# A reordered mixer front, key copies by SBUF transfers, and expert sums opened before the stream

## The chip, the core and the metric

The kernel runs on one core of one Trainium2 chip. Its time is the device time of one execution in microseconds (us), read as the median of a few runs. All data are float32. The engines named below are PE (TensorE, matrix products), DVE (VectorE), ACT (ScalarE), POOL (GpSimd) and SP (SyncE, which here only issues transfers).

## The reference

One decoder block over 256 tokens of 1024 features:

```
proj = rms_norm(x) @ w_in            # [u | q | k | v | q_idx | k_idx | w_idx | g_ssm | g_att]
q, k, q_idx, k_idx = rope(...)
y_ssm = S5 scan of u, gelu, y * sigmoid(y @ w_glu + b_glu)
score = sum over 16 index heads of relu(q_idx . k_idx) * w_idx     # causal, per 128-query block
sel   = top 64 keys of each query; softmax attention over them -> y_att
x = x + (sigmoid(g_ssm) * (y_ssm @ w_proj_ssm) + sigmoid(g_att) * (y_att @ w_proj_attn)) @ w_out
h = rms_norm(x); gates = softmax of the top 4 of 32 router logits
x = x + sum over 32 experts: gate * (clamped swiglu(h @ w_moe_in[e] + b_moe_in[e]) @ w_moe_out[e] + b_moe_out[e])
return rms_norm(x)
```

The expert weights are 32 x 12.6 MB, 403 MB of the 437 MB that the core moves.

## The kernel before, in words

**Layout.** Features lie on the partitions and tokens along the row in the mixer. One tensor `mem` of 24 slots of 8 KB per partition holds the mixer's tiles first and the weights of two experts later; `late`, `xs`, `table` and `bias_rows` lie beside it. PSUM has eight banks: 0 and 1 rotate among the "jobs" of the list `JOBS` (a job's products go to bank job number mod 2, and it waits until the job two before it is evicted); 2 and 3 take the scan's outputs and the attention's; 4 to 7 take scan inputs, index scores, logits, projections and at last the four sums of the expert stage (two token blocks by two feature halves).

**Order.** There is no scheduler: each engine's block is a program written out by hand, and semaphores order the engines. On PE, `x_job` is one chunk of `w_in` (256 columns, 64 matmul records), `score_job` four index heads of one query block, `logits(t)` the attention logits of block t, `turn_prob(t)` the transposes of its probabilities, `attend(t)` its products with v, `ps_job` a quarter of the projection of y_ssm. In the order of PE: `KK`, `QI0` to `QI3`, `VW`, `Q0`, `Q1`, `S0` to `S2`, then the three products `KR0` to `KR2` (L1092) that replicate each 32-row group of the rotated keys `kk` onto four groups of 32 partitions (`krep`), evicted by ACT; `S3` and `A0` with the eight score jobs between their steps; `A1`, `A2`, `logits(0)`, `GLU0/1`, `A3`, `logits(1)`, `PS0/1`, `turn_prob(0)`, `PS2/3`, `attend(0)`, `turn_prob(1)`, `attend(1)`; the attention projection (L1188), the output projection (`W0` to `W7`, L1211) with `aux` products (L1200) that turn the rows token-major and give router logits. DVE makes the scan, the rope, `y_raw` (L745), the index scores (L760, L763), `choose_keys` (eight rounds of max and match_replace, L776 and L777), `mask` (logits plus bias and row maxima, L791 and L794) and `probabilities`. ACT makes the gates, `exponentials` (L478) and most evictions.

**Expert stage.** `one_pass` treats each expert for up to 64 of its tokens: `gather` (L1236, products of `xs` with a one-hot), `gather_t` (L1244, transposes), the inner product (L1277, 64 records with the input bias of L1288), `scatter` of the expert before (L1253) into banks 4 to 7, the gates of the activation, and the outer product (L1325). Weights come in six loads of 2 MB per expert (`load_first` for the first two experts as slots come free, L359 in the loop: a load waits until the chunk two experts earlier has been used, `chunk_used`). In expert 30, L1303 adds the residual with `diag` (a diagonal of the norm's root); in expert 31, L1295 adds the output bias. A branch around further passes (L278) reads the largest number of tokens of an expert from `flag` (L277). Then the final norm is made from banks 4 to 7, and two transfers store the output.

## Time and profile before

| | |
|---|---|
| median of 3 runs | 1170.8 us (1169.01 to 1173.03) |
| the profiled execution's own time | 1169.42 us |
| its span | 1167.6 us |
| PE busy | 1118.3 us (96%), 5578 matmul records |
| DVE, ACT busy | 343.2 us (29%), 157.2 us (13%) |
| moved by the DMA engines | 437.01 MB, mean 374 GB/s |
| expert loads | 192 of 2048 KB |

The profile is of one execution. A busy PE is not PE at its peak, since records cover the wait for operands too. The profile's granted clock is a share of full speed: 1.00 is 2.4 GHz and 0.50 is 1.2 GHz. In a row of the chain or the timeline the first number is the start in us from the span's start and the second the duration; in brackets stands the idle time of the engine before it and what ended it.

### The profile page before, as it was taken

Reading aid. Unit: us, or ns where it says so; the run is one execution under the profiler, and the core shown is the slowest. Engines: PE = TensorE matmul, PEld = TensorE weight load, DVE = VectorE, ACT = ScalarE, POOL = GpSimd, SP = SyncE. Lnnn points to the kernel's source line nnn. Section 1 sums busy time; section 2 is a strip of 40 time slices with the busy share of each in tenths; the row PEclk is TensorE's granted clock in tenths of the full one; section 3 lists DMA queues with packets and bytes.
Section 4 is the critical chain, followed back from the end, with each engine's and each line's share of the span. In section 5 each row is a group of like instructions: output and inputs, shape, how many; then the busy total and the mean of one; then the engine's idle time right before and its main releaser. Section 6 shows DMA issues by size and latency. Waiting matters only on the chain.

```text
span 1167.6 us, 13800 instructions
## 1 busy us (share of the span) xinstructions
PE 1118.3 (96%) x5578; PEld 490.3 (42%) x5578; DVE 343.2 (29%) x760; ACT 157.2 (13%) x331; POOL 0.7 (0%) x7
## 2 busy tenths in 40 slices
PE   9999998989999999999999999999999999999995
PEld 8877786843333333333333333333333333333332
DVE  7999774221112221111111112211111111111112
ACT  2311433130001100010000001000000000000002
POOL 0000000000000000000000000000000000000000
PEclk9999998999999999999999999999999999999999
DMA  8343665589999999999999999999999999999992
GB/s 334 145 145 109 266 261 216 217 321 430 427 427 428 430 428 428 429 428 428 429 429 428 428 430 429 427 429 429 428 428 429 429 427 429 429 429 427 428 429 105
DMA packets 33434, 437.01 MB, mean 374 GB/s; under 512 B 3840, under 2 KB 3968, under 8 KB 5504
## 3 DMA queue, kind: packets, MB, share of 16 engines
q1 hardware_dynamic: 33120, 435.96, 89.1%
q10 hardware_dynamic: 288, 0.69, 0.2%
q8 instruction: 19, 0.31, 0.1%
q14 instruction: 7, 0.06, 0.0%
HBM read 435.58 MB, written 1.05 MB: 374 GB/s over the span
## 4 chain that ended last, share of the span: by engine, by line
PE 63%; DMA 22%; SPq 7%; DVE 6%; issue 1%; ACT 1%; DVEq 0%
PE ps L1277 25%; DMA mem<-in_w_moe 21%; PE ps L1325 13%; PE ps L1010 7%; SPq L359 7%; PE ps L1236 4%; PE ps L1253 3%; DVE mem L574 3%; PE ps L1211 2%; PE ps L1288 2%; PE ps L1188 1%; PE ps L1244 1%; PE ps L1310 1%; PE ps L1056 1%; PE ps L1107 1%
## 5 line engine op out<-in xcount | busy, mean ns | idle before, releaser
L1277 PE MATMUL ps<-mem,late 128*64 128x512 f32 x2048 | 458.2, 595 | 22.9 <-DMA mem<-in_w_moe 22.7
L1277 PEld LDWEIGHTS ps<-mem,late 128*64 128x64 f32 x2048 | 141.6, 137 | 330.7 <-issue 282.3
L1325 PE MATMUL ps<-mem,late 128*64 128x512 f32 x1024 | 226.8, 595 | 0.0
L938 DVE TENSOR_SCALAR late<-ps 128x512 f32<-128x512 f32 x32 | 22.1, 692 | 689.0 <-PE ps L1277 689.0
L1010 PE MATMUL ps<-mem 128*128 128x256 f32 x640 | 143.4, 382 | 0.0
L1010 PEld LDWEIGHTS ps<-mem 128*128 128x128 f32 x640 | 119.9, 190 | 21.0 <-issue 4.5
L1325 PEld LDWEIGHTS ps<-mem,late 128*64 128x64 f32 x1024 | 70.7, 137 | 133.3 <-issue 128.1
L537 ACT ACTIVATE late<-late 128x512 f32<-128x512 f32 x32 | 20.2, 630 | 514.9 <-DVE late L938 514.9
L1253 PE MATMUL ps<-late 64*128 64x512 f32 x256 | 63.6, 615 | 0.8 <-ACT late L544 0.8
L1236 PE MATMUL ps<-xs,late 128*64 128x512 f32 x256 | 63.5, 618 | 0.8 <-DVE late L574 0.8
L574 DVE TENSOR_TENSOR mem<-mem 128x1024 f32<-128x1024 f32 (+8 forms) x89 | 61.2, 729 | 6.5 <-ACT mem L429 3.7
L544 ACT ACTIVATE late<-ps 128x512 f32<-128x512 f32 x32 | 19.1, 597 | 230.7 <-PE ps L1325 230.7
L574 DVE TENSOR_TENSOR late<-late 128x128 f32<-128x128 f32 (+2 forms) x98 | 38.4, 419 | 6.5 <-ACT late L528 0.9
L1253 PEld LDWEIGHTS ps<-late 64*128 64x128 f32 x256 | 22.1, 186 | 41.8 <-issue 41.8
L1288 PE MATMUL ps<-bias_rows,late 32*64 32x512 f32 x256 | 34.8, 613 | 0.0
L574 DVE TENSOR_TENSOR late<-ps,vec 128x512 f32<-128x512 f32 x32 | 22.1, 692 | 41.4 <-PE ps L1244 41.4
L1236 PEld LDWEIGHTS ps<-xs,late 128*64 128x64 f32 x256 | 16.0, 138 | 43.1 <-issue 42.2
L574 DVE TENSOR_TENSOR mem<-ps,mem 128x1024 f32<-128x1024 f32 (+2 forms) x28 | 24.6, 914 | 18.1 <-PE ps L1188 16.9
L533 ACT ACTIVATE late<-ps 128x512 f32<-128x512 f32 x32 | 19.2, 599 | 79.5 <-PE ps L1236 79.5
L1211 PE MATMUL ps<-mem 128*128 128x256 f32 x128 | 28.8, 379 | 0.0
L1211 PEld LDWEIGHTS ps<-mem 128*128 128x128 f32 x128 | 24.0, 190 | 3.0
L1310 PEld LDWEIGHTS ps<-table,late 128*128 128x128 f32 x128 | 13.4, 140 | 28.1 <-issue 24.3
(161 smaller groups left out, 518.9 us busy)
## 6 DMA issues: line engine op xcount, KB each, us to landing
mem<-in_w_moe SPq DMA_DIRECT2D x192, 2048.0 KB, 42.4
mem<-in_w_mix SPq DMA_DIRECT2D x26, 1024.0 KB, 5.4
mem<-in_w_mix SPq DMA_DIRECT2D x2, 512.0 KB, 7.3
out<-xs SPq DMA_DIRECT2D x2, 512.0 KB, 3.1
late<-in_turn_w SPq DMA_DIRECT2D x1, 640.0 KB, 3.9
late<-in_mix_tables SPq DMA_DIRECT2D x1, 576.0 KB, 14.8
mem<-in_x_t ACTq DMA_DIRECT2D x1, 512.0 KB, 4.6
mem<-in_x_t SPq DMA_DIRECT2D x1, 512.0 KB, 5.8
```

Source lines behind the costliest of these rows:

```text
L359: sp.dma_start(place_of(half, n), expert_part(e, n)).then_inc(moe_in[half][n], 16)
L537: ac.activation(sig, gate_z, ACT.Sigmoid, scale=ALPHA).then_inc(sig_ok, 1)
L574: return ve.tensor_tensor(out_, a, b, op)
L938: ve.tensor_scalar(gate_z, z[:, 0], LIMIT, None, ALU.min).then_inc(z_gate, 1)
L1010: i = pe.matmul(b[:, m * T:m * T + T], slot[:, k, first_m + m, :], src[:, k, :], start=(k == 0), stop=(k == kt - 1))
L1211: i = pe.matmul(b[:, 0:T], wide(f"W{m // 2}")[:, k, m % 2, :], mixed[:, k, :], start=(k == 0), stop=(k == KD - 1))
L1236: i = pe.matmul(ps[64 * q:64 * q + SLOTS, 3, :], one_hot[:, t, :], xs[:, t, 512 * q:512 * q + 512], start=(t == 0), stop=(t == TT - 1))
L1253: i = pe.matmul(ps[:, 4 + 2 * t + q, :], gated_t[r, t * P:t * P + P], y_tok[r, :], start=opens, stop=False, skip_group_check=True)
L1277: i = pe.matmul(ps[r, n // 2, :], h_sel[:, k % 4, k // 4, :], w[:, 512 * n:512 * n + 512], start=(k == 0), stop=(k == KD - 1))
L1288: pe.matmul(ps[r, n // 2, :], chosen[g, n, :], b_in[g, :], start=False, stop=False)
L1310: i = pe.transpose(ps[:, 0, n * P:n * P + P], act[:, n * P:n * P + P], ident)
L1325: i = pe.matmul(ps[64 * q:64 * q + SLOTS, 2, :], act_tile(k), w[:, 512 * q:512 * q + 512], start=(k == 0), stop=(k == KF - 1))
```

## The change

1. The products `KR0` to `KR2` and their evictions go. SP copies the groups of `kk` by 12 transfers within SBUF, of 32 partitions by 2 KB, after `roped` 1 and before the load of `A2`; `score_job(0)` waits for the four of group 2, `logits(0)` for the other eight.
2. New order. The score jobs begin one step later and end in `A1`; `y_raw` comes after the scores on DVE; `logits(0)` and `logits(1)` come before and after `A2`; `turn_prob(0)` before `A3`; `attend(0)`, `turn_prob(1)` between the last `ps_job`s. `choose_keys(1)` is cut in two around `probabilities(0)`. The mask, exponentials and probabilities of block 1 go in two halves of four heads. All four `PS` evictions are made by DVE. `attend(1)` is in two halves, and the projection's first four outputs in two passes over k.
3. Opened sums. `aux` rows are kept unscaled in `raw`; four products with the identity put the residual into banks 4 to 7 before the expert loop (three of them before `picked_ok` is awaited, one after the first `gather_t`), so `diag` and L1303 go. The output bias goes into expert 1 (four products of 32 rows) and L1295 goes. `gates_turned` stands before `gather_t`. The load of chunk 5 waits for these.
4. Tail. `flag` is read at the start of the loop on each engine; ACT loads the root's table under the last outer product; the norm's mean and root are made per token block, and the last scaling of block 1 is shared by ACT and DVE.

The three places of PE's order that the prediction speaks of follow. First, behind `S2` (feature products are L1010 before and L1046 now; the key copies L1092; score jobs L1107 and L1135). Before:

```order
L1056 MATMUL ps<-mem 32x256 x16
L1010 MATMUL ps<-mem 128x256 x16
L1092 MATMUL ps<-mem,late 128x256 x6
L1010 MATMUL ps<-mem 128x256 x4
L1107 MATMUL ps<-mem 128x128 x8
```

Now:

```order
L1092 MATMUL ps<-mem 32x256 x16
L1046 MATMUL ps<-mem 128x256 x24
L1135 MATMUL ps<-mem 128x128 x8
L1046 MATMUL ps<-mem 128x256 x4
L1135 MATMUL ps<-mem 128x128 x8
```

The six key products are gone, and half of `S3` (eight instructions more in the row of feature products) comes ahead of the first score job; L1092 is now the scan's output.

Second, from the last scan output to the projection (L1124 and L1152 logits, L1136 and L1164 transposed probabilities, L1147 and L1175 products with v, L1188 and L1216 projection). Before:

```order
L1056 MATMUL ps<-mem 32x256 x16
L1010 MATMUL ps<-mem 128x256 x32
L1124 MATMUL ps<-mem 128x128 x16
L1010 MATMUL ps<-mem 128x256 x32
L1124 MATMUL ps<-mem 128x256 x16
L1010 MATMUL ps<-mem 128x256 x16
L1136 MATMUL ps<-table,xs 128x128 x8
L1010 MATMUL ps<-mem 128x256 x16
L1147 MATMUL ps<-mem 64x128 x8
L1136 MATMUL ps<-table,xs 128x128 x16
L1147 MATMUL ps<-mem 64x128 x16
L1188 MATMUL ps<-mem 128x256 x32
```

Now:

```order
L1152 MATMUL ps<-mem 128x128 x16
L1046 MATMUL ps<-mem 128x256 x16
L1152 MATMUL ps<-mem 128x256 x16
L1046 MATMUL ps<-mem 128x256 x16
L1164 MATMUL ps<-table,xs 128x128 x8
L1046 MATMUL ps<-mem 128x256 x32
L1175 MATMUL ps<-mem 64x128 x8
L1046 MATMUL ps<-mem 128x256 x8
L1164 MATMUL ps<-table,xs 128x128 x16
L1046 MATMUL ps<-mem 128x256 x8
L1175 MATMUL ps<-mem 64x128 x16
L1216 MATMUL ps<-mem 128x256 x32
```

Both blocks of logits now stand 16 or more feature products earlier, and the last `ps_job` stands between the transposes and the products with v of block 1.

Third, the start of the expert stage (L1219 and L1269 the slots' prefix sums, L1236 and L1286 gather, L1226 and L1276 the gates' transposes, L1244 and L1294 gather_t, L1262 now the opened sums). Before:

```order
L1200 MATMUL ps<-late,mem 128x160 x4
L1219 MATMUL ps<-late,table 128x64
L1220 MATMUL ps<-late,table 128x32
L1236 MATMUL ps<-xs,late 64x512 x4
L1244 MATMUL ps<-table,late 128x128 x4
L1226 MATMUL ps<-table,late 64x128 x2
L1227 MATMUL ps<-late,table 128x32
L1228 MATMUL ps<-late,table 128x32
L1277 MATMUL ps<-mem,late 64x512 x4
```

Now:

```order
L1241 MATMUL ps<-late,mem 128x160 x4
L1262 MATMUL ps<-mem,table 128x512 x3
L1269 MATMUL ps<-late,table 128x64
L1270 MATMUL ps<-late,table 128x32
L1286 MATMUL ps<-xs,late 64x512 x4
L1276 MATMUL ps<-table,late 128x128 x2
L1277 MATMUL ps<-late,table 128x32
L1278 MATMUL ps<-late,table 128x32
L1294 MATMUL ps<-table,late 128x128 x4
L1262 MATMUL ps<-mem,table 128x512
L1327 MATMUL ps<-mem,late 64x512 x4
```

Three opened sums stand where PE waited for the router, the gates' transposes moved ahead of `gather_t`, and the fourth sum stands ahead of the first inner product.

The diff, cut to what the prediction speaks of:

```diff
...
-JOBS = ["U0", "U1", "KK", "QI0", "QI1", "QI2", "QI3", "VW", "Q0", "Q1", "S0", "S1", "S2", "KR0", "KR1", "KR2", "S3",
-        "A0", "A1", "A2", "GLU0", "GLU1", "A3", "PS0", "PS1", "P0_0", "P0_1", "PS2", "PS3"] \
-    + [f"P1_{n}" for n in range(4)] + [f"W{m}" for m in range(KD)]
...
+JOBS = ["U0", "U1", "KK", "QI0", "QI1", "QI2", "QI3", "VW", "Q0", "Q1", "S0", "S1", "S2", "S3",
+        "A0", "A1", "A2", "GLU0", "GLU1", "P0_0", "P0_1", "A3", "PS0", "PS1", "PS2"] \
+    + [f"P1_{n}" for n in range(4)] + ["PS3"] + [f"W{m}" for m in range(KD)]
...
-            one_pass(0, 0)
-            eng.wait_ge(flag_ok, 1)
-            most = eng.value_load(flag[0:1, 0:1], min_val=0, max_val=T)
+            held = []
+            def most_tokens():
+                eng.wait_ge(flag_ok, 1)
+                held.append(eng.value_load(flag[0:1, 0:1], min_val=0, max_val=T))
+            one_pass(0, 0, most_tokens)
+            most = held[0]
...
+            sp.wait_ge(roped, 1)
+            for n in (2, 0, 1):
+                for a in range(4):
+                    sp.dma_start(krep[32 * a:32 * a + 32, n], kk[32 * n:32 * n + 32]).then_inc(krep_in[n], 16)
+            load("A2")
...
-            sp.wait_ge(rstd_ok, 1)
+            sp.wait_ge(opened, 1)
+            sp.wait_ge(x_norm, TT)
             load_first(5)
...
-            relus(0, 1, 2)
+            relus(0, 1)
             gate("S", gate_s, V_BG, 3)
             ac.wait_ge(roped, 3)
-            relus(3, 4, 5, 6)
+            relus(2, 3, 4, 5)
             gate("A", gate_a, V_BG + KD, 0)
-            relus(7)
...
+            relus(6, 7)
...
+            ready(ACT.Exp)
+            exponentials(0, 1, 0, NH)
...
-            exponentials(0)
+            prob_turned(0)
+            ready(ACT.Exp)
+            for n in range(2):
+                exponentials(1, 2 + n, 4 * n, 4 * n + 4)
...
-            for n in range(2):
-                evict(f"PS{n}", p_ssm[:, 2 * n:2 * n + 2, :], pair)
-            prob_turned(0)
-            exponentials(1)
-            attended(0)
+            attended(0, 1, 2, slice(0, 4))
             prob_turned(1)
-            attended(1)
+            attended(1, 2, 3, slice(0, 2))
+            attended(1, 3, 2, slice(2, 4))
...
-                for t in range(TT):
-                    ac.activation(at(10 * SW + P * (TT * m + t), P), b[:, t, 0:P], ACT.Square,
-                                  accum_out=stat[:, 64 + KD * t + m:65 + KD * t + m]).then_inc(squared1, 1)
-                ac.activation(xs[:, :, m * P:m * P + P], b[:, :, 0:P], ACT.Copy).then_inc(tok_ok, 1)
+                ac.activation(raw[:, :, m * P:m * P + P], b[:, :, 0:P], ACT.Copy).then_inc(tok_ok, 1)
...
-            ac.wait_ge(var_f_ok, 1)
-            ac.activation(stat[:, 4:6], stat[:, 2:4], ACT.Sqrt).then_inc(root_f_ok, 1)
-            ac.wait_ge(rstd_f_ok, 1)
+                if n % 2:
+                    t = n // 2
+                    ac.wait_ge(mean_f_ok, t + 1)
+                    ac.activation(stat[:, 4 + t:5 + t], stat[:, t:t + 1], ACT.Sqrt, scale=1.0 / D,
+                                  bias=stat[:, 46:47]).then_inc(root_f_ok, 1)
+            ac.wait_ge(rstd_f_ok, 2)
             ac.wait_ge(under_gains, 4)
-            ac.activation(final[:, 1, :], final[:, 1, :], ACT.Copy, scale=stat[:, 7:8]).then_inc(out_ready[1], 1)
+            ac.activation(final[:, 1, 0:512], final[:, 1, 0:512], ACT.Copy, scale=stat[:, 7:8]).then_inc(
+                out_ready[1], 1)
...
+            ve.wait_ge(y_done, 4)
+            for a in range(KS):
+                i = ve.scalar_tensor_tensor(y_raw[:, a, :], u_in[:, a, :], vec[:, V_D + a:V_D + a + 1],
+                                            ps[:, 2 + a // 2, (a % 2) * T:(a % 2) * T + T], ALU.mult, ALU.add)
+            i.then_inc(y_raw_ok, 1)
+            choose_keys(0, 0, NSEL // 8)
+            mask(0, 0, NH)
+            choose_keys(1, 0, 5)
+            probabilities(0, 1, 0, NH)
+            choose_keys(1, 5, NSEL // 8)
             ve.wait_ge(*evicted("GLU1"))
             ve.wait_ge(*evicted("GLU0"))
             tt(y_ssm, y_gelu, glu_g, ALU.mult).then_inc(y_ssm_ok, 1)
-            choose_keys(1)
-            probabilities(0)
-            ve.wait_ge(*evicted("PS1"))
-            ve.wait_ge(*evicted("PS0"))
-            tt(p_ssm[:, 0:4, :], p_ssm[:, 0:4, :], gate_s[:, 0:4, :], ALU.mult)
-            mask(1)
+            for n in range(2):
+                mask(1, 4 * n, 4 * n + 4)
+            for n in range(2):
+                probabilities(1, 2 + n, 4 * n, 4 * n + 4)
             ve.wait_ge(rout_in, 16)
             tt(turn_w[:, :, P:P + NE], turn_w[:, :, P:P + NE],
                vec[:, V_G2:V_G2 + KD].unsqueeze(2).to_broadcast([P, KD, NE]), ALU.mult).then_inc(w_gain, 1)
-            for n in (2, 3):
+            for n in range(4):
                 ve.wait_ge(rot_done, JOB[f"PS{n}"] + 1)
...
                 ins.then_inc(route_ok, 1)
             def gates_out():
-                for t in range(TT):
-                    ins = ve.tensor_scalar(diag[:, t, :], ident, stat[:, 4 + t:5 + t], None, ALU.mult)
-                ins.then_inc(diag_ok, 1)
...
                 ve.tensor_copy(stat[:, 62:63], stat[:, 60:61])
             passes(ve, one_pass)
-            ve.tensor_copy(stat[:, 63:64], stat[:, 60:61]).then_inc(tile_ok, 1)
...
             for n, bank_free in ((1, None), (0, (squared, 1)), (3, (sum_ok, 1)), (2, (squared, 3))):
+                if n == 3:
+                    ve.wait_ge(squared, 2)
...
                    ALU.mult).then_inc(under_gains, 1)
+            ve.wait_ge(root_f_ok, 1)
+            ve.reciprocal(stat[:, 6:7], stat[:, 4:5]).then_inc(rstd_f_ok, 1)
...
-            ve.tensor_scalar(stat[:, 2:4], stat[:, 0:2], 1.0 / D, EPS, ALU.mult, ALU.add).then_inc(var_f_ok, 1)
-            ve.wait_ge(root_f_ok, 1)
-            ve.reciprocal(stat[:, 6:8], stat[:, 4:6]).then_inc(rstd_f_ok, 1)
+            tt(stat[:, 1:2], stat[:, 50:51], stat[:, 51:52], ALU.add).then_inc(mean_f_ok, 1)
             ve.wait_ge(rstd_f_ok, 1)
             ve.wait_ge(under_gains, 4)
             ve.tensor_scalar(final[:, 0, :], final[:, 0, :], stat[:, 6:7], None, ALU.mult).then_inc(out_ready[0], 1)
+            ve.wait_ge(root_f_ok, 2)
+            ve.reciprocal(stat[:, 7:8], stat[:, 5:6]).then_inc(rstd_f_ok, 1)
+            ve.wait_ge(rstd_f_ok, 2)
+            ve.tensor_scalar(final[:, 1, 512:D], final[:, 1, 512:D], stat[:, 7:8], None, ALU.mult).then_inc(
+                out_ready[1], 1)
...
-            pe.wait_ge(roped, 1)
-            for n in range(3):
-                b = job(f"KR{n}")
-                r = slice(32 * n, 32 * n + 32)
-                for half in range(2):
-                    i = pe.matmul(b[:, half * T:half * T + T], sel[r, :], kk[r, half, :], start=True, stop=True)
...
-                    pe.wait_ge(*evicted("KR2"))
+                    pe.wait_ge(krep_in[2], 64)
...
             def turn_prob(t):
-                pe.wait_ge(prob_ok, t + 1)
                 for n in range(2 * (t + 1)):
...
+            def scores_from(first):
+                return lambda step: score_job(first + step) if 0 <= first + step < 8 else None
+            x_job("S3", between=scores_from(-1))
+            x_job("A0", between=scores_from(3))
             y_out(3)
-            x_job("A1")
-            pe.wait_ge(tables_in, 16)
+            x_job("A1", between=scores_from(7))
+            logits(0)
             x_job("A2")
-            logits(0)
+            logits(1)
             chunk_arrived(pe, "GLU")
             pe.wait_ge(gelu_ok, 1)
             for n in range(2):
                 feature_job(f"GLU{n}", y_gelu, KS, 2 * n, deep("GLU"))
+            pe.wait_ge(tables_in, 16)
+            turn_prob(0)
             x_job("A3")
-            logits(1)
             pe.wait_ge(y_ssm_ok, 1)
             ps_job(0)
             ps_job(1)
-            turn_prob(0)
+            attend(0, 2, range(NH))
             ps_job(2)
+            turn_prob(1)
             ps_job(3)
-            attend(0)
-            turn_prob(1)
-            attend(1)
-            pe.wait_ge(att_out, 2)
-            pe.wait_ge(row_max, 2)
-            for m in range(KD):
-                if m % 4 == 0:
-                    chunk_arrived(pe, f"PA{m // 4}")
-                if m >= 4:
-                    pe.wait_ge(gated_a, m - 3)
+            attend(1, 3, range(4))
+            pe.wait_ge(att_out, 1)
+            attend(1, 2, range(4, NH))
+            def project(m, ks):
                 slot = deep(f"PA{m // 4}")
-                for k in range(KS):
+                for k in ks:
                     i = pe.matmul(ps[:, 4 + m % 4, (m // 4) * T:(m // 4) * T + T], slot[:, k, m % 4, :],
                                   y_att[:, k, :], start=(k == 0), stop=(k == KS - 1))
-                i.then_inc(proj_done, 1)
+                return i
+            chunk_arrived(pe, "PA0")
+            pe.wait_ge(row_max, 3)
+            pe.wait_ge(att_out, 2)
+            for m in range(4):
+                project(m, range(2))
+            pe.wait_ge(att_out, 3)
+            for m in range(4):
+                project(m, range(2, KS)).then_inc(proj_done, 1)
+            chunk_arrived(pe, "PA1")
+            for m in range(4, KD):
+                pe.wait_ge(gated_a, m - 3)
+                project(m, range(KS)).then_inc(proj_done, 1)
...
+            open_sums(0, 0)
+            open_sums(1, 0)
+            open_sums(0, 1)
...
-                            pe.matmul(ps[:, 4 + k, :], gates_t[r, t * P:t * P + P], b_out[r, :], start=False,
-                                      stop=False, skip_group_check=True)
+                        if out_bias and k == 0:
+                            pe.wait_ge(gates_t_ok, 1)
+                            for n in range(4):
+                                r = slice(NE * n, NE * n + NE)
+                                pe.matmul(ps[:, 4 + n, :], gates_t[r, n // 2 * P:n // 2 * P + P], b_out[r, :],
+                                          start=False, stop=False, skip_group_check=True)
                     if not head:
-                        scatter(j - 1, opens=opens)
-                        if adds:
-                            pe.wait_ge(diag_ok, 1)
-                            for t in range(TT):
-                                for q in range(2):
-                                    pe.matmul(ps[:, 4 + 2 * t + q, :], diag[:, t, :], xs[:, t, 512 * q:512 * q + 512],
-                                              start=False, stop=False, skip_group_check=True)
+                        scatter(j - 1)
                     if not tail:
                         gather(j + 1)
...
+                if isinstance(c, int):
+                    gates_turned()
                 gather_t(first)
                 if isinstance(c, int):
-                    gates_turned()
+                    open_sums(1, 1).then_inc(opened, 1)
                 pairs = c * (NE // 2)
...
+                body(first + 1, pairs, 1, out_bias=isinstance(c, int))
+                if most_tokens:
+                    most_tokens()
                 with pe.Fori(1, NE // 2 - 1) as m:
                     for odd in range(2):
                         body(2 * m + (first + odd), m + pairs, odd)
-                body(first + NE - 2, pairs + NE // 2 - 1, 0, adds=isinstance(c, int))
+                body(first + NE - 2, pairs + NE // 2 - 1, 0)
                 body(first + NE - 1, pairs + NE // 2 - 1, 1, tail=True)
                 pe.wait_ge(gated_t_ok, first + NE)
                 scatter(first + NE - 1, first_sum_ok)
...
```

## Rows read from the trace of the kernel before

**Rows 1.** Timeline of SP's queue, first issue of the expert loop.
```profile
258.72 37.19 SPq L359 DMA_DIRECT2D mem<-in_w_moe  x10
```

**Rows 2.** Windows: each engine's busy us, granted clock, DMA share, GB/s.
```profile
300.00:700.00 400.00, 400.00 (x1924) 135.19 (x1926) 71.16 (x171) 34.62 (x58) 0.00 (x0) 1.00 1.01 428
188.00:192.00 4.00, 3.45 (x16) 2.67 (x14) 0.00 (x0) 2.31 (x4) 0.00 (x0) 0.50 1.01 426
248.00:250.00 2.00, 1.93 (x6) 0.78 (x8) 0.99 (x6) 0.96 (x3) 0.00 (x0) 0.50 1.05 451
```

**Rows 3.** The chain that ended last: start us, us, what; its middle.
```profile
181.02 4.05 ACT xs L478 x16
...
1056.54 48.09 DMA mem<-in_w_moe
1104.68 3.65 PE ps L1277 x16
```

**Rows 4.** The same chain, from expert 30's residual to the end.
```profile
1110.25 3.63 PE ps L1303 x8
...
1124.12 1.72 PE ps L1277 x8
...
1126.85 1.05 PE ps L1295 x2
...
1136.66 7.04 PE ps L1277 x32
...
1147.89 7.08 PE ps L1325 x32
...
1157.73 2.28 issue
```

**Rows 5.** PE's timeline before the expert stage.
```profile
109.27 2.94 PE L1092 MATMUL ps<-mem,late 32*128 32x256 f32 x12
...
134.47 1.93 PE L1056 MATMUL ps<-mem 128*32 128x256 f32 x32
...
182.92 1.09 PE L1147 MATMUL ps<-mem 128*64 128x128 f32 x16
187.68 3.77 PE L1136 MATMUL ps<-table,xs 128*128 128x128 f32 x16 [3.67 <-DVE xs L574]
192.23 3.71 PE L1147 MATMUL ps<-mem 128*64 128x128 f32 x32 [0.78 <-ACT mem L429]
196.62 14.08 PE L1188 MATMUL ps<-mem 128*128 128x256 f32 x64 [0.69 <-ACT mem L488]
...
246.63 0.43 PE L1219 MATMUL ps<-late,table 128*128 128x64 f32 x2 [3.64 <-DVE late L865]
...
248.07 3.51 PE L1236 MATMUL ps<-xs,late 128*64 128x512 f32 x8 [0.81 <-DVE late L574]
```

**Rows 6.** DVE's timeline, from y_raw to the mask of block 1.
```profile
136.54 1.66 DVE L745 SCALAR_TENSOR_TENSOR mem<-mem,vec,ps 128x256 f32<-128x256 f32 x4 [8.10 <-PE ps L1056]
...
148.57 0.29 DVE L574 TENSOR_TENSOR mem<-mem,late 128x128 f32<-128x128 f32 x1
...
156.74 1.22 DVE L794 TENSOR_REDUCE stat<-xs 128x8 f32<-128x1024 f32 x1
...
160.67 0.42 DVE L574 TENSOR_TENSOR mem<-mem,late 128x256 f32<-128x256 f32 x1
...
169.66 0.43 DVE L574 TENSOR_TENSOR mem<-mem,late 128x256 f32<-128x256 f32 x1
...
176.38 2.28 DVE L791 SCALAR_TENSOR_TENSOR xs<-ps,mem 128x2048 f32<-128x2048 f32 x1
```

**Rows 7.** ACT's timeline: the last relu of the scores.
```profile
134.60 1.02 ACT L464 ACTIVATE mem<-ps 128x1024 f32<-128x1024 f32 x1 [0.27 <-PE ps L1107]
```

**Rows 8.** The branch of PE around further passes: ns min/median/max, start.
```profile
L278 PEldq COMPARE_BRANCH  x1: 3312/3312/3312, 1156.6 to 1156.6; - x1
```

**Rows 9.** DMA issues: count, KB each, median us from issue to landing.
```profile
mem<-in_w_mix SPq DMA_DIRECT2D x26, 1024.0 KB, 5.4
```

169 lines of the change are left out of this document (87 added, 82 removed).

## The prediction

> **What bounds the kernel now.** I read the windows first, then the chain that ended last, then PE's timeline up to the expert stage, then DVE's. In the window 300 to 700 us both PE and the DMA engines are full, the latter at 428 GB/s [rows 2]. The chain tells which of them sets the end: near it, PE waits for a load of expert weights that lands at 1056.54 + 48.09 = 1104.63 us [rows 3]. A load of 2.097 MB at 428.5 GB/s takes 4.89 us. The loop's first load is issued at 258.72 [rows 1]; the one of 1104.63 (chunk 3 of expert 30) is the 172nd, and 258.72 + 172 x 4.89 = 1100, plus some 4 us from issue to landing. So from the first used chunk on the stream is back to back: the end is the moment at which PE uses its first chunk, plus a stream of fixed length, plus what PE does after the last landings. Whatever brings the first inner product forward by one microsecond brings the end forward by one; work taken from PE in the middle brings nothing; work taken from PE behind 1104.63 counts as far as the loads let it.
>
> Behind 1104.63 the chain is PE's own until the norm [rows 4]. The loads of expert 31 land 4.89 apart: its chunk 0 at about 1119.3, chunk 3 at 1134.0, chunk 5 at 1143.8.
>
> Ahead of the stream PE is without a gap up to 174 us, and then loses time in one place: it waits 3.67 for the probabilities of block 1, then its granted clock is 0.50 (1.2 GHz), then it waits 0.78 and 0.69 for evictions [rows 2, 5]. A second place is the router: a wait of 3.64, then a first gather at half clock [rows 2, 5]. DVE, on whose work the first wait rests, sat idle for 8.10 us before `y_raw` [rows 6].
>
> **Front: keys and order.** The key products leave PE: 2.9 us [rows 5]. Their replacement is 12 transfers of 64 KB. SP is free for them at about 101 us, when the first rope ends, behind the load of `A1`. The nearest row is 1 MB in 5.4 us [rows 9]; 12 x 64 KB is 0.79 MB, so I take 6 to 8 us: landed at 107 to 109. The first score job wants group 2 at 109.3 plus half a chunk, 16 records of 0.22 = 3.5 (0.22 is 14.08 / 64 [rows 5]), so 113; the logits want the rest at 141. The next load of SP, `A2`, waits for `S2` until 109.3 anyway. Cost nothing, with about 4 us of cover; beyond that each microsecond costs one. Bounds: 0, and the row of 5.4 us for each transfer, one after another: 12 x 5.4 = 65, the last landed at 166, 25 us too late for `logits(0)`. I take 0, because transfers overlap in the queue: a load that is 48.09 us under way [rows 3] has others landing every 4.89.
>
> DVE is idle from 136.54 - 8.10 = 128.4 because `y_raw` stands ahead of the scores. Now the scores start there and end 2.6 (a quarter of the 10.4 between 138.2 and 148.57 [rows 6]) after the last relu. That relu started at 134.60 [rows 7]; it gains 2.9 by the keys but the last score job now comes behind y_out (1.93, [rows 5]) and a quarter of `A1` (1.8): it starts at 135.5, ends at 136.5; scores end at 139.1, `y_raw` (1.66) at 140.8. Selection and mask of block 0 took from 148.57 to 156.74 + 1.22 = 157.96 [rows 6], 9.4 us; so they end at 150.2, 7.8 us earlier. PE reaches `logits(1)` at 148.8 and waits 1.4 there for bank space: the one new wait. DVE then needs 9.4 (160.67 to 170.09 [rows 6]) for the selection of block 1, 1.5 for `probabilities(0)`, 1.2 for y_ssm, 4.9 for two mask halves: 167.3. The exponentials (4.05 for eight heads [rows 3], now two times 2) overlap the halves, and the last probabilities are ready at 170.8. PE asks for them at 179.7, so the wait of 3.67 goes, with 9 us of cover. Evictions of ACT lie beside PE; I walked them one by one, and they leave 0.3 us in `turn_prob(0)` and 0.8 in `turn_prob(1)`.
>
> Without the long wait the clock should stay at 2.4 GHz. At 1.2 GHz the products with v took 3.71 for 32 records, against 1.09 for 16 at 2.4 GHz, so 2.2 for 32: 1.5 lost; the transposes took 3.77, of which 1.4 by the same share [rows 2, 5]. Sum up to the projection: 2.9 (keys) + 3.7 (wait) + 2.9 (clock) + 1.5 (two eviction waits) - 1.4 - 1.1 = 8.5 us; the projection starts at 188.1 instead of 196.62 [rows 5]. The first four outputs of the projection come in two passes, but DVE's gating still keeps ahead of PE. All loads that wait on these events shift with them.
>
> **Front: opened sums.** Three of the four identity products (0.9 each, as L1303 took 3.63 for four [rows 4]) fill the 3.64 us of waiting for the router; they cost nothing and keep PE at work. The gather then should take 1.9, not 3.51: 1.6 gained. But `gates_turned` (0.75) now stands ahead of `gather_t` and must wait for four gate copies, and the fourth sum (0.9) stands ahead of the first inner product, beside the eviction by DVE (0.7) that this waits for: 0.6 back. Net 1.0 us; between -0.2 (clock still low) and 1.6.
>
> The Trainium skill (TensorE: Matmul & The Clock Gate, "What's actually happening") says that the throttled clock is the default and activity releases it. This trace agrees in direction: 0.50 after the idle stretches, 1.00 before them [rows 2]. By it the gather would get the 1.6; a trace of an engine with short gaps there is not in this profile, so the sum above keeps the rest as a bound.
>
> The load of chunk 5 is issued 9 us later in relation to the gather, but it is the sixth of an expert and wanted 20 us later; it lands just when the stream begins, so no hole opens. The output bias adds 1.0 to expert 1, and the reading of `flag` some 0.8 on PE, both in the part of the stream where PE is ahead of the loads: nothing.
>
> **End of the stream.** L1303 (3.63) and the four L1295 (4 x 1.05) leave PE behind 1104.63, 7.8 us. PE would be ready for expert 31 at 1124.12 - 3.63 = 1120.5, its chunk 0 has landed at 1119.3. Steps of 1.8 bring it to chunk 3 at 1132.7, which lands only at 1134.0; two steps (3.65 [rows 3]) more, and the inner product ends at 1137.65, not 1136.66 + 7.04 = 1143.70 [rows 4]. 6.0 us gained, 1.8 kept by the loads. Chunk 5 (1143.8) is wanted at 1145.4: it doesn't bind. Bounds: 4.5 if landings are 1.5 later than I extrapolate, 7.8.
>
> **Tail.** The wait of 2.28 us before the last two sums [rows 4] looks like the reading of `flag`, but the long part is PE's branch, 3.31 us from 1156.6 [rows 8], and the branch stays. Only the read ahead of it goes, some 0.7: between 0 and 0.7, as the branch may wait for the last products; I take 0.4. If the branch was long only because of the read, 2.3. The divided last scaling and the mean per block give 0.2. Together 0.6.
>
> **Sum.** 8.5 + 1.0 + 6.0 + 0.6 = 16.1 us. The profiled execution took 1169.42: 1153.3. It lies 1.4 below the median of the runs, 1170.8, which would give 1154.7. I predict 1154.0.
>
> **Rivals.**
> - The chain through DVE and ACT is later than I walked it (evictions in the new order block a bank, halves cost more than their share): the front gives 4 instead of 8.5, so 1158.5. For it: PE has only two rotating banks. Against it: 9 us of cover in the longest chain.
> - The clock falls anyway, in the new wait at 149 or a later one. Before, a half-clock stretch followed a wait of 3.67, and the following work cost 2.9 more [rows 5]; with a full chunk of feature products at half clock it costs up to 5: 1159. Against it: no wait above 1.4 remains.
> - The stream does not start earlier: the loads of the first two experts, which come free with the mixer's tiles, are late. Then only 6.6 stand: 1164. Against it: the DMA engines have 50 us for the nine last loads, 44 us of work, and those keep their distance to the events.
> - PE's branch shortens with the read: 2 us more, 1152, and with the loads slightly earlier 1150.
> - Slower: the 12 small transfers land one after another, each at more than the 1 MB load's time. The last eight hold `logits(0)`, wanted at 141. The kernel is 3.5 us slower than before once they land 16.1 + 3.5 = 19.6 later than that, at 160.6: twelve in 59.6 us, 5.0 each. At 5.4 each [rows 9] it would be 1154.0 + 25 = 1179. Against it: overlap in the queue, as above, and a row that has 16 times the bytes.
>
> On that last one, the Trainium skill (DMA: Bandwidth & Descriptors, "Rules for kernel authors") warns that many small transfers are mostly overhead below 64 KB, and its section on the anatomy of one DMA gives about 2 us fixed. Estimated from that page, twelve one after another would need 24 us and land at 125, inside the cover; no row here has a transfer within SBUF. It speaks against the change, without reaching the price.
>
> **Chances.** The forecast (1151.5 to 1157) 0.60; late evictions 0.14; clock 0.08; no earlier stream 0.04; shorter branch 0.11; slower 0.03. The likeliest is 1154.0. The range from 1150 to 1161 takes in the branch, the late evictions and the clock. Within 0.3% (3.5 us, about what a measurement can tell from no change) of 1170.8 lies none of the cases, only the edge of the third: 0.02. Faster 0.95, slower 0.03.
>
> **What would show it.** In the changed profile: PE's projection starts at about 188, the first inner product at about 244.2, the loop's first load near 249; no window at 0.50 between 150 and 250; the transposes of block 1 not waiting for DVE; in the chain a wait for a load of expert 31, and its inner product ending some 3.7 after that load; no L1303, L1295 behind it; PE's branch still of 2.5 to 3.3 us. I am wrong if the first score job waits for a transfer, if the distance from the first loop load to the end isn't shorter by 6 to 7 us, or if a half-clock stretch appears.

## The result, and the profile after

The changed kernel takes 1152.9 us (median; 1152.16 to 1153.64), against 1170.1 (1169.01 to 1173.03) for the kernel before, measured beside it: a ratio of 0.9847, 95% interval 0.9829 to 0.9865. The forecast was 1154.0 us, with a range of 1150 to 1161. The profiled execution took 1152.54, with a span of 1150.7; of before the two were 1169.42 and 1167.6.

Two points cut both spans in three: L, the issue of the expert loop's first load, and S, the start of the last scatter. The first row of the table is a part of the second.

| | before | after | change | predicted |
|---|---|---|---|---|
| projection starts | 196.62 | 187.69 | -8.93 | -8.5 |
| L | 258.72 | 248.47 | -10.25 | -9.5 |
| S - L | 897.02 | 891.59 | -5.43 | -6.0 |
| span - S | 11.86 | 10.64 | -1.22 | -0.6 |
| sum of the last three | | | -16.9 | -16.1 |

PE's timeline of the changed kernel up to the stream (start, length, instructions; in brackets the idle time before them and what ended it) answers to [rows 5]:

```profile
113.06 0.71 PE L1135 MATMUL ps<-mem 32*128 32x128 f32 x14 [0.27 <-issue]
...
150.03 2.01 PE L1152 MATMUL ps<-mem 32*128 32x256 f32 x32 [1.05 <-DVE stat L816]
...
160.20 0.63 PE L1164 MATMUL ps<-table,xs 128*128 128x128 f32 x4 [0.58 <-ACT mem L513]
...
180.29 1.06 PE L1164 MATMUL ps<-table,xs 128*128 128x128 f32 x8 [0.44 <-DVE mem L601]
181.69 0.63 PE L1164 MATMUL ps<-table,xs 128*128 128x128 f32 x4 [0.34 <-ACT mem L444]
...
187.69 1.13 PE L1216 MATMUL ps<-mem 128*128 128x256 f32 x4
...
237.57 0.43 PE L1269 MATMUL ps<-late,table 128*128 128x64 f32 x2 [0.95 <-DVE late L896]
...
239.02 1.94 PE L1286 MATMUL ps<-xs,late 128*64 128x512 f32 x8 [0.81 <-DVE late L601]
...
243.46 1.94 PE L1327 MATMUL ps<-mem,late 128*64 128x512 f32 x8
```

The wait of 3.67 us for the probabilities is gone and the longest left is 1.05, in front of the second block's logits; at the router 0.95 is left of 3.64. L1216 is the projection, L1286 the gather, L1327 the first inner product. The same windows as in [rows 2] now have a granted clock of 1.00 where 0.50 stood (the last number but two), and the stream's rate is unchanged. That the clock had been full ahead of the wait for the probabilities, which [rows 2] don't show, stands in the first row here, of the kernel before; the other three are of the changed kernel:

```profile
180.00:184.00 4.00, 4.00 (x30) 3.13 (x28) 2.61 (x4) 2.98 (x13) 0.00 (x0) 1.00 0.56 139
...
188.00:192.00 4.00, 4.00 (x20) 3.53 (x19) 0.00 (x0) 1.66 (x3) 0.00 (x0) 1.00 1.06 440
248.00:250.00 2.00, 2.00 (x12) 0.72 (x10) 0.00 (x0) 0.00 (x0) 0.00 (x0) 1.00 0.99 426
300.00:700.00 400.00, 400.00 (x1926) 135.58 (x1926) 74.91 (x180) 35.42 (x59) 0.00 (x0) 1.00 1.01 428
```

The chain that ended last answers to [rows 3] and [rows 4]:

```profile
1074.64 49.60 DMA mem<-in_w_moe
...
1124.28 3.68 PE ps L1327 x16
...
1127.98 0.69 DVE late L966
...
1132.15 7.09 PE ps L1367 x32
...
1140.06 1.99 PE ps L1303 x8
1142.05 1.76 issue
```

The last load for which PE waits is now chunk 3 of expert 31, in place of chunk 3 of expert 30, and the inner product ends 3.7 us after it landed. Behind it are neither identity nor bias products. Ahead of it, the chain is PE's own work from 262 us up to 743; only behind that does it run through loads. What PE waits for loads in the whole stream (us in total, times, longest) is

```profile
PE ps L1327 <- DMA mem<-in_w_moe: 24.2, 26, 1.2
```

and the first of these waits ends at 766.85. Up to there PE uses chunks that have landed before it asks for them, although the stream runs at 428 GB/s all the time. The kernel before has 22.7 us of such waits, the first ending at 752.30. Last, SP's queue, which answers to [rows 1], and the SBUF transfers (count, KB each, median us from issue to landing):

```profile
100.88 8.46 SPq L325 DMA_DIRECT2D mem<-mem  x12
109.39 0.58 SPq L302 DMA_DIRECT2D mem<-in_w_mix  x1
...
202.72 41.17 SPq L309 DMA_DIRECT2D mem<-in_w_moe  x6
248.47 50.42 SPq L373 DMA_DIRECT2D mem<-in_w_moe  x12
```

```profile
mem<-mem SPq DMA_DIRECT2D x12, 64.0 KB, 2.7
```

### The profile page after: what moved, and what is told of

It is laid out like the page before. It is cut to its first block, busy times and chain, and to the rows that moved or that the text cites. A ratio compares the mean times of both kernels' runs of the same rounds, so it can differ in the third digit from the quotient of the medians.

```text
span 1150.7 us, 13804 instructions
## 1 busy us (share of the span) xinstructions
PE 1106.9 (96%) x5566; PEld 484.6 (42%) x5566; DVE 343.9 (30%) x766; ACT 156.4 (14%) x332; POOL 0.7 (0%) x8
## 3 DMA queue, kind: packets, MB, share of 16 engines
HBM read 435.52 MB, written 1.05 MB: 379 GB/s over the span
## 4 chain that ended last, share of the span: by engine, by line
PE 54%; DMA 26%; DVE 6%; SPq 4%; issue 1%; ACT 1%; ACTq 0%
DMA mem<-in_w_moe 26%; PE ps L1327 25%; PE ps L1367 12%; SPq L373 4%; PE ps L1303 3%; PE ps L1286 3%; PE ps L1046 2%; PE ps L1252 2%; DVE mem L601 2%; PE ps L1338 2%; PE ps L1216 1%; PE ps L1294 1%; PE ps L1352 1%; DVE mem L784 1%; DVE xs L601 1%
## 5 line engine op out<-in xcount | busy, mean ns | idle before, releaser
L1327 PE MATMUL ps<-mem,late 128*64 128x512 f32 x2048 | 457.7, 595 | 24.2 <-DMA mem<-in_w_moe 24.2
L1327 PEld LDWEIGHTS ps<-mem,late 128*64 128x64 f32 x2048 | 141.8, 137 | 332.5 <-issue 280.6
L1046 PE MATMUL ps<-mem 128*128 128x256 f32 x640 | 143.5, 382 | 0.0
L1046 PEld LDWEIGHTS ps<-mem 128*128 128x128 f32 x640 | 119.8, 190 | 20.5 <-issue 4.1
L1303 PE MATMUL ps<-late 64*128 64x512 f32 x256 | 63.6, 615 | 0.9 <-ACT late L562 0.9
L1286 PE MATMUL ps<-xs,late 128*64 128x512 f32 x256 | 61.9, 604 | 0.8 <-DVE late L601 0.8
L1303 PEld LDWEIGHTS ps<-late 64*128 64x128 f32 x256 | 22.1, 186 | 41.9 <-issue 41.9
L1286 PEld LDWEIGHTS ps<-xs,late 128*64 128x64 f32 x256 | 15.7, 136 | 42.4 <-issue 41.5
L1352 PEld LDWEIGHTS ps<-table,late 128*128 128x128 f32 x128 | 13.4, 140 | 28.1 <-issue 24.4
```

Of the source, the lines that this page charges most:

```text
L1046: i = pe.matmul(b[:, m * T:m * T + T], slot[:, k, first_m + m, :], src[:, k, :], start=(k == 0), stop=(k == kt - 1))
L1286: i = pe.matmul(ps[64 * q:64 * q + SLOTS, 3, :], one_hot[:, t, :], xs[:, t, 512 * q:512 * q + 512], start=(t == 0), stop=(t == TT - 1))
L1303: i = pe.matmul(ps[:, 4 + 2 * t + q, :], gated_t[r, t * P:t * P + P], y_tok[r, :], start=False, stop=False, skip_group_check=True)
L1327: i = pe.matmul(ps[r, n // 2, :], h_sel[:, k % 4, k // 4, :], w[:, 512 * n:512 * n + 512], start=(k == 0), stop=(k == KD - 1))
L1352: i = pe.transpose(ps[:, 0, n * P:n * P + P], act[:, n * P:n * P + P], ident)
```

## The experiments

Twelve runs follow: ten variants of the changed kernel, one of the kernel before, and the changed kernel again. A difference in microseconds is taken from medians (1152.9 for the changed kernel, 1153.4 in the last series), the place of it from L and S of one profiled execution each. The runs come from three chips, on which the kernel before has medians of 1169.6, 1171.3 and 1171.2, and only the last series has the changed kernel beside it; so in the other two a difference of medians is known to about 1 us only.

S - L needs the same care. The changed kernel itself has 891.59 and 892.42 in two executions, and variants whose work behind L is that of the changed kernel have up to 893.50. All of that arises ahead of the last load that PE waits for: once PE has begun on that chunk (1124.28 above), S comes 15.8 us later in each of those looked at. To compare kernels whose work near the end differs, I therefore measure from an earlier point that all but one of them share, the start of the products that wait for chunk 3 of expert 30. In the changed kernel these are

```profile
1094.76 3.65 PE L1327 MATMUL ps<-mem,late 128*64 128x512 f32 x16 [1.24 <-DMA mem<-in_w_moe]
```

and S comes 45.3 us after their start (45.1 to 45.6 in the kernels with the same code there); in the kernel before it comes 51.1 us after 1104.68.

**Key products back.**

```diff
-            for n in (2, 0, 1):
-                for a in range(4):
-                    sp.dma_start(krep[32 * a:32 * a + 32, n], kk[32 * n:32 * n + 32]).then_inc(krep_in[n], 16)
+            for n in range(3):
+                b = job(f"KR{n}")
+                ...
```

> The changed kernel with the key copies made by three products and their evictions again, in place of the transfers. My theory: PE is without a gap there, so 2.9 us come back in full: projection start 187.7 + 2.9 = 190.6, first loop load near 251.4, time 1152.9 + 2.9 = 1155.8. Rival (the products hide in the new wait of 1.05 us at the second logits, because DVE's selection, not PE, sets row_max): +1.9 or less, 1154.8. Rival (transfers disturb the loads): no difference, 1152.9.

Measured: 1155.5 (1155.24 to 1156.06), ratio 0.9873 [0.9856, 0.9889]. L is 251.19, 2.72 later; PE's waits are the same, the one of 1.05 now at 152.72. The projection starts at 190.38, 2.69 later: in the new order the products cost what they take on PE, 2.94 less the 0.27 that PE waits there without them. The time agrees with the theory (1155.8), and the transfers disturb no load enough to be seen.

**The transfers alone, in the kernel before.**

```diff
-            for name in CHUNKS[CHUNK["QI1"]:CHUNK["GLU"]]:
+            for name in CHUNKS[CHUNK["QI1"]:CHUNK["A2"]]:
                 load(name)
+            sp.wait_ge(roped, 1)
+            for n in (2, 0, 1):
+                ...
+            load("A2")
-            (the products KR0 to KR2 and their evictions)
```

> The kernel before with one part of the change alone: the twelve SBUF transfers in place of the six replicating products and their three evictions; order, sums and tail as before. If the products simply stand in TensorE's sequence, as the prediction priced them (-2.9 us), the time is 1167.3 us and the first load of the expert loop is issued at 255.8 in place of 258.7. Rival: in the order of before TensorE only waits longer for the probabilities of block 0 (3.67 us at 187.7 before), and the gain is under 1 us: 1169.5 to 1170.5.

Measured: 1169.4 (1166.63 to 1170.97, 10 runs), ratio 0.9984 [0.9972, 0.9995]: 1.8 us less than the 1171.2 of the kernel before beside it (the interval has 0.6 to 3.3), between the two theories, and neither had the reason. PE's timeline of this kernel:

```profile
113.10 0.73 PE L1103 MATMUL ps<-mem 32*128 32x128 f32 x16 [2.02 <-issue]
...
186.71 1.09 PE L1132 MATMUL ps<-table,xs 128*128 128x128 f32 x8 [3.67 <-DVE xs L578]
...
195.19 5.01 PE L1184 MATMUL ps<-mem 128*128 128x256 f32 x22 [0.69 <-ACT mem L492]
```

The first score product would be due 2.94 us earlier than the 114.07 of before; it starts at 113.10. In the kernels of the new order with early transfers it starts at 112.9 to 113.3 too. It needs the rotated index queries as well, and DVE's timeline has their last step end just there:

```profile
108.38 4.62 DVE L578 TENSOR_TENSOR mem<-ps,mem 128x1024 f32<-128x1024 f32 x4
113.03 2.36 DVE L578 TENSOR_TENSOR mem<-mem 128x1024 f32<-128x1024 f32 x2
```

In the changed kernel the same step ends at 108.34 + 4.62 = 112.96 and the first score product starts at 113.06, again 0.1 behind. So of 2.94 us 0.97 arrives. In the changed kernel that product stands one quarter of a chunk later (8 products, 1.99 us), and the wait is 0.27. The new order is what lets the transfers pay: at the projection they bring 1.43 us here and 2.69 there. The rest of the stage is as before, the wait of 3.67 included. The projection is 1.43 earlier, but this execution then lost it again: its clock was at half from 246 to 256 us, where the profile of before has 248 to 251.4, and it issued its first load at 259.61, 0.9 later than before.

**Transfers behind the load of A2.**

```diff
+            load("A2")
             sp.wait_ge(roped, 1)
             for n in (2, 0, 1):
                 ...
-            load("A2")
```

> The changed kernel with the twelve transfers issued behind the load of A2, from 109.9 us instead of 100.9. My theory: at 0.59 us per issue and 2.7 to 5 to landing, group 2 lands at 109.9 + 4 x 0.59 + 2.7 to 5 = 115 to 117.3 and the first score job, ready at 113.06, waits 2 to 4: that comes back in full, time 1155 to 1157. Rival (DVE's selection sets the pace and takes it up): 1152.9 to 1153.9.

Measured: 1159.3 (1157.12 to 1160.22), ratio 0.9892 [0.9862, 0.9922]. SP issues the transfers from 109.72 on, not 100.88, and PE's timeline shows

```profile
116.71 1.24 PE L1135 MATMUL ps<-mem 32*128 32x128 f32 x16 [3.94 <-DMA mem<-mem]
```

So the fourth transfer landed 4.6 us after its issue at about 112.1. In the changed kernel the fourth is issued at 103.2: by the same 4.6 us that is some 5 us of cover (predicted: about 4). This takes the load of A2, which is issued just ahead here, to have slowed nothing; the median from issue to landing is 3.4 here and 2.7 there. Once it is gone the price is above one for one: L is 6.13 later for 3.67 us more of waiting. The 16 products took 1.24 in place of 0.73, and the clock was at half for 6.8 us, from 115.0, still within the wait, to 122. I had expected 2 to 4 of waiting, which came, and nothing beyond it, which was wrong.

**y_raw ahead of the scores again.**

```diff
-            scores()
             (y_raw, four instructions)
+            scores()
```

> The changed kernel with y_raw ahead of the index scores on DVE again. My theory: DVE waits for the last scan output until 132.4, so the scores start at 134.1 and not at 128.45, and end 10.4 later at 144.5 and not at 139.0; y_raw no longer stands behind them, so row_max of block 0 comes 3.8 later, at 153.8. PE waits 4.9 there in place of 1.05, and its granted clock then goes to 0.50 for a while, which costs another 2 to 5: time 1152.9 + 3.8 + 3 = 1160, between 1156.7 and 1162. Rival (the clock stays): 1156.7. Rival (later covers take up the delay): 1152.9.

Measured: 1158.8 (1158.22 to 1159.91), ratio 0.9894 [0.9866, 0.9922]. The wait of 1.05 becomes

```profile
154.25 3.50 PE L1152 MATMUL ps<-mem 32*128 32x256 f32 x32 [5.02 <-DVE stat L816]
```

3.97 more of waiting, 1.49 for 32 products at half clock (2.01 at full), and L is 5.85 later. The theory had 4.9 for this wait and 1160 for the time. This is the half of the new order that moves DVE's work into its own idle time of [rows 6].

**No overlap of exponentials and mask halves.**

```diff
-                exponentials(1, 2 + n, 4 * n, 4 * n + 4)
+                exponentials(1, 3, 4 * n, 4 * n + 4)
```

(and the same for the probabilities on DVE)

> The changed kernel, but the exponentials of block 1 wait for both mask halves, and the probabilities for both halves of exponentials, so nothing overlaps. My theory: probabilities end at about 173.5 in place of 170.3; PE asks for them at 179.2: no difference, 1152.9. Only the projection evictions of DVE move. Rival (the halving is part of the gain): +2 to +3, 1155 to 1156.

Measured: 1155.6 (1154.96 to 1156.59), ratio 0.9862 [0.9834, 0.9889]; L is 2.07 later. My theory of no difference fell, and the rival's size (2 to 3) came true. PE's and ACT's timelines in this kernel:

```profile
173.08 3.29 PE L1046 MATMUL ps<-mem 128*128 128x256 f32 x14 [1.74 <-ACT mem L453]
```

```profile
170.89 1.28 ACT L453 ACT_TABLE_LOAD   x1
172.19 0.84 ACT L453 ACTIVATE mem<-ps,vec 128x256 f32<-128x256 f32 x2
```

ACT stands in one sequence: the gate of A3 comes behind block 1's exponentials, and holds the bank that the next product writes. In the changed kernel this gate starts at 170.12, 2.07 earlier, and PE doesn't wait. So its cover there is 2.07 - 1.74 = 0.33 us. The 9 us that I gave to this chain are true of the probabilities, not of the eviction behind them. This execution also has S - L at 893.50, 1.9 longer than the changed kernel with the same code: near the end PE waited 2.54 us for a load (1.24 in the changed kernel), and the 16 products behind it took 5.35 at half clock in place of 3.65. That is the spread spoken of above, and nothing of this edit.

**The sums opened late, and once more with idle products in the gap.** The first variant adds the four identity products in expert 30. The second does the same, and fills PE's gap at the router with three products whose result nobody uses.

```diff
-            open_sums(0, 0)
-            open_sums(1, 0)
-            open_sums(0, 1)
+            (second variant) pe.matmul(ps[:, 4 + 2 * t + q, :], ident, raw[:, t, 0:512], start=True, stop=True)
...
+                        if adds: ...
+                                    pe.matmul(ps[:, 4 + 2 * t + q, :], ident, xs[:, t, 512 * q:512 * q + 512], ...
```

> The changed kernel without the opened sums; four products with the identity over the normalised rows stand in expert 30 in their place (so the residual is of the wrong scale; the cost is that of before). My theory: behind the stream +1.9 (3.63 less what the loads cover); at the router PE waits some 3.7 us again, its granted clock goes to 0.50, the first gather takes 3.5 and not 1.9, but the fourth sum (0.9) is gone from the path: front +1.6 - 0.9 = +0.7. Time 1155.5. Rival (the clock has nothing to do with the three sums): gather 1.9, front -0.9, time 1153.9.

> The kernel of the run before this one (residual in expert 30) with three products of the same size as the opened sums put into the wait for the router; their results are thrown away. My theory: only PE's being at work counts for the clock, so the gather takes 1.9 again and the first loop load comes 1.6 us earlier than in the run before; time 1153.9. Rival: no difference from that run.

Measured: 1154.8 (1154.62 to 1155.46), ratio 0.9869 [0.9853, 0.9886], and 1154.2 (1153.52 to 1154.44), 0.9863 [0.9847, 0.9879]. PE's timelines at the router, first without products in the gap, then with idle ones:

```profile
237.73 0.69 PE L1259 MATMUL ps<-late,table 128*128 128x64 f32 x2 [3.53 <-DVE late L895]
...
239.60 3.47 PE L1276 MATMUL ps<-xs,late 128*64 128x512 f32 x8 [0.81 <-DVE late L600]
...
245.20 1.08 PE L1317 MATMUL ps<-mem,late 128*64 128x512 f32 x4 [0.78 <-DVE late L600]
```

```profile
237.49 0.43 PE L1265 MATMUL ps<-late,table 128*128 128x64 f32 x2 [0.96 <-DVE late L896]
...
238.94 1.94 PE L1282 MATMUL ps<-xs,late 128*64 128x512 f32 x8 [0.81 <-DVE late L601]
```

L is 250.22 in the one and 248.39 in the other, against 248.47 in the changed kernel. The two differ only in work that yields nothing, so in this pair of profiles what the opened sums bring at the front is the clock, and all of it: 1.8 us. The medians of the two, from one chip, are only 0.7 apart. The mean granted clocks of the single executions point to a reason: 0.995 or 0.996 in all four without products in the gap, but 0.999, 0.998, 0.996 and 0.996 with them. So products in the gap seem not to keep the clock up in every execution; only the first of these has a profile.

The fourth sum, which I had priced at 0.6, cost nothing: the variants without it wait 0.78 there for DVE's eviction instead. At the end the two variants agree: S comes 46.5 us after the products that wait for chunk 3 of expert 30, against 45.3 in the changed kernel. So the identity products in expert 30 cost 1.2 us (0.8 to 1.3 against all kernels with the changed kernel's code), where I had expected 1.9.

**Output bias of expert 31.**

```diff
-                body(first + NE - 1, pairs + NE // 2 - 1, 1, tail=True)
+                body(first + NE - 1, pairs + NE // 2 - 1, 1, tail=True, out_bias=isinstance(c, int))
```

> The changed kernel with the output bias again in expert 31 (four products of 1.05 us, 4.2 in all). My theory: part of it is covered by the loads of expert 31, so the inner product of expert 31 ends at 1124.12 - 3.63 + (1143.70 - 1124.12) = 1140.1 in the time of before, 2.4 later than 1137.7: the inner product ends about 2.4 after that of the changed kernel relative to the first loop load, time 1155.3, and no wait for chunk 3 of expert 31 remains. Rival (nothing behind the last load wait is covered): +4.2, 1157.1. Rival (all covered): 1152.9.

Measured: 1155.4 (1154.68 to 1157.25), ratio 0.9878 [0.986, 0.9896]. The theory had 1155.3. L is the same (+0.12) and S - L 2.44 longer. From the products that wait for chunk 3 of expert 30 (at 1095.12 in this kernel) S comes 47.5 us later, 2.2 more than in the changed kernel (1.9 to 2.4 against all kernels with its code), so this is not the spread of the stream. PE waits for no load behind 1095.12: its own work ends last again, as before.

**More work inside the loop.** One more product of 512 columns per expert, result unused.

```diff
+                    pe.matmul(ps[:, 3, :], ident, xs[:, 0, 0:512], start=True, stop=True)
```

> The changed kernel with one more product of 128x512 (0.9 us) ahead of each gather, 32 in all, 29 us of PE; their results are overwritten. My theory: between the first expert and the last, the loads set the pace (4.89 per load, 29.4 per expert, against some 27.1 of PE), so all but the first (on the way to the stream, +0.9) hide: first loop load +0.9, time 1153.8, and the chain reaches back to a load earlier than before. Rival (PE sets the pace for most of the stream, as its share of 100% suggests): +29 less what the waits for loads hold (24 us), or more: 1160 to 1182.

Measured: 1155.7 (1154.64 to 1156.52), ratio 0.9867 [0.9839, 0.9895]. The added products cost 2.8; S - L grew by 1.7, L by 0.5. But my theory fell, for in this kernel the loads don't set the pace any more: PE waits for no load at all, and the chain has none in the whole stream. An expert takes PE 28.1 us, against 27.1 in the changed kernel, so some 31 us of work were added between L and S, and what PE loses to the loads in the changed kernel hid all but 1.7 of it: the 24.2 us of waits, and some 5 more around them (from the gather of expert 2 to that of expert 31 that kernel takes 812.2 us, 27.4 more than 29 times 27.06, and 2.5 more lie behind it). The rival had this mechanism, and with 1160 too high a price. So PE's work in the loop is free only as long as these waits hold, for about 0.9 us in each expert.

**PE's branch.** The further passes over the experts, which this input does not need, are left out on PE.

```diff
-            passes(pe, one_pass)
+            one_pass(0, 0)
```

> The changed kernel with the further passes over the experts, and the branch that skips them, left out on TensorE alone; with this input they don't run. In the changed kernel TensorE's branch takes 3.66 us at 1140.1 and the final products start 1.76 us after what they wait for. Theory: the products start 1.8 us earlier and the end comes 1.8 us earlier (1151.1 us). Rival: the squares and the root on ScalarE, which go on beside the branch, end last then, and only about 0.5 us is gained (1152.4 us).

Measured: 1153.3 (1152.54 to 1153.96, 4 runs), against 1153.4 (1152.66 to 1154.46) for the changed kernel beside it; ratios 0.985 [0.9836, 0.9865] and 0.9852 [0.9839, 0.9865]. PE's wait of 1.79 is gone, the last ACT step starts 5.68 after S instead of 6.40, and 0.7 us of a trace don't show in the medians, which are 0.1 apart. My theory (1.8 us) fell; as in the rival, ACT's squares and root, two blocks of them, end last once PE does not. The changed kernel's own branch is

```profile
L284 PEldq COMPARE_BRANCH  x1: 3656/3656/3656, 1140.1 to 1140.1; - x1
```

**The changed kernel again, and an order beyond it.**

```diff
-            logits(1)
...
-            for n in range(2):
-                feature_job(f"GLU{n}", y_gelu, KS, 2 * n, deep("GLU"))
+            feature_job("GLU0", y_gelu, KS, 0, deep("GLU"))
+            logits(1)
+            feature_job("GLU1", y_gelu, KS, 2, deep("GLU"))
```

(also: the second product of PS0 behind the first block's attention product; ACT's gate of A2 ahead of the first exponentials)

> The changed kernel once more, unaltered, on the chip of the three other kernels of this series, so that differences of one microsecond can be read. Expected: 1152.9 us, 0.985 of the kernel before; first load of the expert loop at 248.5.

> An attempt at a better version. In the changed kernel TensorE waits 1.05 us for the maximum of block 0's logits (at 150.0) and 0.58 us for the exponentials (at 160.2). Here the second block's logits move between the two halves of the GLU product, so that VectorE gets its job earlier relative to TensorE's need, and the second block's probability product goes behind the first block's attention product; ScalarE evicts the gate of A2 ahead of block 0's exponentials. Theory: the 1.05 us and some 0.3 us of the 0.58 go, nothing new waits: 1151.6 us, first load at 247.1. Rival: ScalarE, which is the one with least room there (A3's gate ends 0.2 us ahead of its need), takes the gain back: 1152.9 us or up to 1 us more.

Measured: 1153.4 (1152.66 to 1154.46), ratio 0.9852 [0.9839, 0.9865], and 1151.2 (1150.98 to 1152.42), ratio 0.9837 [0.9824, 0.9849]. Every run of the new variant lies below every run of the changed kernel. PE's timeline of it:

```profile
152.43 2.01 PE L1152 MATMUL ps<-mem 32*128 32x256 f32 x32
...
159.11 0.63 PE L1164 MATMUL ps<-table,xs 128*128 128x128 f32 x4 [0.59 <-ACT mem L513]
```

The wait of 1.05 is gone, that of 0.59 is not, and L is 247.41: 1.06 gained, of the 1.3 expected, with nothing new in the way. The medians differ by 2.2. The rest lies in what the profiled execution of the changed kernel shows in this series: its gather falls to half clock.

```profile
239.04 2.74 PE L1286 MATMUL ps<-xs,late 128*64 128x512 f32 x8 [0.81 <-DVE late L601]
```

Its windows, granted clock in the last column but two:

```profile
236.00:239.00 3.00, 1.27 (x6) 0.52 (x4) 2.16 (x14) 2.98 (x3) 0.00 (x0) 1.00 0.99 426
239.00:241.00 2.00, 1.96 (x8) 0.58 (x8) 0.97 (x6) 0.94 (x3) 0.00 (x0) 0.76 1.05 451
241.00:243.00 2.00, 2.00 (x9) 1.29 (x8) 0.37 (x3) 1.17 (x2) 0.00 (x0) 0.50 0.99 426
```

L was 249.59 there, 1.1 later than in the first profile of the very same kernel, and that execution is the slowest of its five. The profile of the kernel without PE's branch, whose front is the same, has the half clock at the gather too (L 249.56). Executions of equal mean clock can be compared: at 0.998 the spans are 1150.8, 1150.9 and 1151.5 in three of the five of the changed kernel, and 1149.1, 1149.4, 1149.4 and 1149.6 in four of the five of the new order. So most of the 2.2 us, about 1.5, is the order, and the rest goes with executions of a lower mean clock, two of five against one of five. Whether the better order keeps the clock up more often can't be told from five executions each.

## Why the prediction was right

**Front (predicted 8.5 up to the projection and 1.0 behind it, measured 8.9 and 1.3).** The keys brought 2.7 of 2.9, but only with the new order; my sum had them as products in PE's sequence and did not ask what else the first score job waits for. It came out right by luck, because the same diff moved that job by a quarter of a chunk. The wait of 3.67 went, the wait ahead of the second logits came (1.05 for 1.4), and the evictions left 0.58, 0.44 and 0.34 where I had 0.3 and 0.8. That the half clock follows a long wait was shown in both directions: putting a wait of 3.9 or 5.0 back brings it back and costs 1.9 to 2.5 us beyond the wait, and in the profiled pair idle products in a gap take it away. The opened sums' share was right in direction; its parts were off on both sides: the clock brings 1.8, where I had 1.6, and the 0.6 taken back by the fourth sum does not exist, since it lies beside DVE's eviction. The measured 1.3 holds for executions in which the gather keeps the full clock. In two of the ten profiles with the opened sums at the router, one of them the second of the changed kernel, it fell to half clock all the same, L came 1.1 later, and the share was 0.2. So one of the three signs of being wrong that the prediction names, a half-clock stretch, is there in some executions, with no wait above 1.05 us ahead of it; my rival "the clock falls anyway" holds for them at a price of 1.1, not 5. The Trainium skill (TensorE: Matmul & The Clock Gate, "What's actually happening") has the full clock released by activity; the pair of variants at the router agrees, 3.47 against 1.94 us for the same eight products. The gathers of 2.74 us with the sums in the gap show that it doesn't settle every execution.

**End of the stream (6.0, measured 5.4).** The mechanism is the one described: load, then 3.68, then nothing but DVE. The landing that ends the wait came 875.77 after L, where my landings of 4.89 from 1104.63 to 1134.0 have 875.28, and this 0.5 is most of what the term is too large by. It is also within the spread of the stream, in which the same landing came up to 877.7 after L (the variant without overlap); the second profile of the changed kernel gives 4.6 for the term. Free of that spread, from the products that wait for chunk 3 of expert 30, the gain is 51.1 - 45.3 = 5.8. Undone alone, the bias costs 2.2 of it and the identities 1.2, each against a term of its own (4.2 and 3.6) of which the loads hide the rest; the two together left PE behind 7.8 us less work, of which the loads kept 2.1, where I had 1.8.

**Tail (0.6, measured 1.2).** PE's branch stayed, with 3.66 us at 1140.1 where [rows 8] have 3.31, and the wait went from 2.28 to 1.76: 0.5 where I had 0.4. The other 0.7 is what remains for the divided scaling and the mean per block, which were put at 0.2; no run takes these apart.

**What was wrong without hurting.** For "1.00 before" the idle stretches the prediction names [rows 2], which have no window there; the window of 180 to 184 us above has it. "9 us of cover" for block 1's probabilities left out that ACT's next eviction stands in the same sequence; cover of an engine's work is the smallest over all that stands behind it. And the price of the slower rival, one microsecond per microsecond of late transfers, is too low, since the wait brings half clock with it. The estimate of 24 us for twelve transfers in a row was worked out from the Trainium skill (DMA: Bandwidth & Descriptors, "Anatomy of one DMA — SWDGE (gpsimd) path"), which fits about 2 us of fixed cost to each transfer that GpSimd issues. Here, issued by SP, they overlap: all are issued within 8.5 us, and each landed after 2.0 to 4.9 us, with a median of 2.7.

Undone one by one, the parts cost 2.6 us (keys), 1.9 (sums), 2.5 (bias), 2.7 (halves) and 5.9 (`y_raw`), each to about 1 us. They don't add up to shares: up to the projection the transfers bring 1.4 in the old order and 2.7 in the new. The rest of the new order (the places of the logits, the transposes and the products with v, and the evictions given to DVE) was not undone by itself.
